# Norm factors by square root and reciprocal in place of logarithm and exponential, at the end and in the linear attention of a two-block model

## The reference, cut to what matters

```python
def rmsnorm(x, g):
    xf = x.astype(jnp.float32)
    y = xf * lax.rsqrt(jnp.mean(xf * xf, axis=-1, keepdims=True) + EPS)
    return (y * g.astype(jnp.float32)).astype(x.dtype)

# in bidirectional_gla, the linear attention (4 heads, 128 values each)
o = (fwd + bwd).astype(v.dtype).transpose(0, 2, 1, 3)
o = rmsnorm(o, norm_g) * jax.nn.silu(r.reshape(B, T, GLA_HEADS, GLA_DV))

# the end of second_block
h = h + sqrelu_mlp(h, ln_ff_g[l], w_ff1[l], w_ff2[l])
return rmsnorm(h, ln_final_g)
```

## Time and profile before

| | before |
|---|---|
| time, median of 3 runs | 2974.15 us (2974.0 to 2974.2) |
| profiled execution, its time | 2975.5 us |
| profiled execution, its span | 2973.7 us |
| mean granted TensorE clock | 0.99 of full speed |
| instructions | 42637 |

### The profile page before, as it was taken

One profiled execution on the slowest core, in us unless ns is written; L12 is line 12 of the kernel. 1 busy time (PEld: TensorE's weight loads), 2 busy tenths in 40 slices (PEclk: granted clock), 3 DMA queues, 4 the chain that ended last, 5 costly groups with the idle time before them and its releaser, 6 DMA issues.

```text
span 2973.7 us, 42637 instructions
## 1 busy us (share of the span) xinstructions
PE 2909.8 (98%) x16332; PEld 2413.5 (81%) x16332; DVE 1984.1 (67%) x3262; ACT 1441.8 (48%) x2411; POOL 467.7 (16%) x764
## 2 busy tenths in 40 slices
PE   9999999889999999999999999999999999999998
PEld 6888888778988887888878888777877788888887
DVE  6653246766775349999989852475654877778864
ACT  4552125887776126555444431375643544444432
POOL 0110004765554120000000010261012000000000
PEclk9999997999999999999999999999999999999999
DMA  4222231000000511333344332000101244464232
GB/s 150 73 84 71 85 114 43 2 1 2 2 2 7 207 43 64 114 114 114 114 160 157 116 111 92 28 2 36 43 30 72 104 165 168 157 241 156 99 114 71
DMA packets 85383, 262.14 MB, mean 88 GB/s; under 512 B 10448, under 2 KB 13648, under 8 KB 84800
## 3 DMA queue, kind: packets, MB, share of 16 engines
q1 hardware_dynamic: 74208, 219.29, 20.3%
q0 software_dynamic: 10976, 40.15, 3.8%
HBM read 187.58 MB, written 66.06 MB: 85 GB/s over the span
## 4 chain that ended last, share of the span: by engine, by line
PE 89%; DVE 4%; ACT 4%; issue 2%; POOL 0%; DMA 0%; SPq 0%; ACTq 0%; DVEq 0%; POOLq 0%
PE PS L256 33%; PE PS L3136 23%; PE PS L3158 12%; PE PS L919 3%; PE PS L933 3%; PE PS L905 2%; PE PS L904 2%; PE PS L280 1%; PE PS L1563 1%; PE PS L1598 1%; PE PS L1585 1%; ACT P_SHORT L1003 1%; PE PS L956 1%; PE PS L3187 1%; ACT PT L1013 1%
## 5 line engine op out<-in xcount | busy, mean ns | idle before, releaser
L223 ACT CAST WHI<-RAW 128x1024 fp32r<-128x1024 f32 x100 | 104.8, 1049 | 589.4 <-PE PS L256 569.6
L228 DVE TENSOR_TENSOR WLO<-RAW,WHI 128x1024 fp32r<-128x1024 f32 x102 | 125.5, 1231 | 361.4 <-ACT WHI L223 360.1
L256 PE MATMUL PS<-HLO,WHI 128*128 128x512 f32 x992 | 306.2, 390 | 0.0
L3136 PE MATMUL PS<-XSH_T,PWH 128*128 128x512 f32 x596 | 233.1, 391 | 5.4 <-DVE PWL L2396 2.4
L3136 PE MATMUL PS<-XSH_T,PWL 128*128 128x512 f32 x596 | 231.9, 389 | 0.0
L3136 PE MATMUL PS<-XSL_T,PWH 128*128 128x512 f32 x596 | 231.9, 389 | 0.0
L3158 PE MATMUL PS<-DXH,PWH 128*128 128x512 f32 x560 | 218.1, 389 | 1.4 <-DVE DXL L2620 1.3
L256 PEld LDWEIGHTS PS<-HLO,WHI 128*128 128x128 f32 x992 | 186.5, 188 | 39.2
L3158 PE MATMUL PS<-DXL,PWH 128*128 128x512 f32 x560 | 217.9, 389 | 0.0
L3158 PE MATMUL PS<-DXH,PWL 128*128 128x512 f32 x560 | 217.9, 389 | 0.0
L3136 PE MATMUL PS<-XSH_B,PWL 128*128 128x512 f32 x456 | 177.4, 389 | 0.0
(11 more groups left out here) (443 smaller groups left out, 7225.6 us busy)
## 6 DMA issues: line engine op xcount, KB each, us to landing
W<-in_w SPq DMA_DIRECT2D x57, 1024.0 KB, 6.4
RAW<-in_w SPq DMA_DIRECT2D x104, 512.0 KB, 3.3
hidden<-W SPq DMA_DIRECT2D x54, 512.0 KB, 2.8
DXR<-hidden_t SPq DMA_DIRECT2D x20, 1024.0 KB, 5.1
DXR<-hidden SPq DMA_DIRECT2D x15, 1024.0 KB, 5.1
hidden_t<-W SPq DMA_DIRECT2D x24, 512.0 KB, 3.3
hidden_t<-T SPq DMA_DIRECT2D x16, 512.0 KB, 3.1
PLAIN_RAW<-hidden SPq DMA_DIRECT2D x14, 512.0 KB, 4.2
```

Source lines behind the costliest of these rows:

```text
L223: nc.scalar.copy(WHI[:, slot, :], RAW[:, slot, :]).then_inc(w_hi, 1)
L228: nc.vector.tensor_tensor(WLO[:, slot, :], RAW[:, slot, :], WHI[:, slot, :].bitcast(F32), ALU.subtract).then_inc(w_lo, 1)
L256: last = nc.tensor.matmul(o[:, half], w[:, slot, cols], x(k)[:, half], start=(k == 0 and w is WHI and x is hi), stop=(done and k == kcs - ...
L3136: last = nc.tensor.matmul(c.banks[q % 2][b], wt[n % 4][:, cols], xt[x][:, k, :], start=(opens and k == 0 and xt is c.xsh and wt is c.pwh), ...
```

## The change

At both places Ln and Exp are replaced by one square root on ScalarE and a reciprocal on VectorE. In linear attention the reciprocal goes ahead of the norm's multiplication, in place, 128x8 elements, and a wait of VectorE for itself follows (`seq`). At the end it goes to the head of `dve_end_scale`, 128x512 or 128x256 elements. The other norms of the kernel keep Ln and Exp.

```diff
@@ act_gla
             act.wait_ge(gl_ms, h + 1)
-            nc.scalar.activation(ORS[:, h, :], OSUM[:, h, :], ACT.Ln, scale=1.0 / GLA_DV, bias=EPS_T[:, 0:1])\
+            nc.scalar.activation(ORS[:, h, :], OSUM[:, h, :], ACT.Sqrt, scale=1.0 / GLA_DV, bias=EPS_T[:, 0:1])\
                 .then_inc(gl_root, 1)
-            act.wait_ge(gl_root, 2 * h + 1)
-            nc.scalar.activation(ORS[:, h, :], ORS[:, h, :], ACT.Exp, scale=-0.5).then_inc(gl_root, 1)
@@ dve_gla_norm
-        dve.wait_ge(gl_root, 2 * h + 2)
+        dve.wait_ge(gl_root, h + 1)
+        seq(dve, nc.vector.reciprocal(ORS[:, h, :], ORS[:, h, :]))
@@ act_ff2_down
             act.wait_ge(mean_done, 4 + i + 1)
-            nc.scalar.activation(LN_B[:, a0:a1], SIDE[0][:, a0:a1], ACT.Ln, bias=EPS_T[:, 0:1]).then_inc(ln_done, 1)
-            act.wait_ge(ln_done, 4 + i + 1)
-            nc.scalar.activation(RSTD[4][:, a0:a1], LN_B[:, a0:a1], ACT.Exp, scale=-0.5).then_inc(rstd_done, 1)
+            nc.scalar.activation(LN_B[:, a0:a1], SIDE[0][:, a0:a1], ACT.Sqrt, bias=EPS_T[:, 0:1]).then_inc(ln_done, 1)
@@ dve_end_scale
         a0, a1 = END_COLS[i]
+        dve.wait_ge(ln_done, 4 + i + 1)
+        nc.vector.reciprocal(RSTD[4][:, a0:a1], LN_B[:, a0:a1]).then_inc(rstd_done, 1)
         dve.wait_ge(rstd_done, 4 + i + 1)
```

## The result

| | before | after |
|---|---|---|
| time, median of 18 runs each | 2975.26 us (2972.35 to 2978.66) | 2980.57 us (2979.0 to 2985.05) |
| ratio | | 1.0021, 95% interval 1.0015 to 1.0027 |
| profiled execution, its time and its span | 2975.5, 2973.7 us | 2982.74, 2981.0 us |
| instructions | 42637 | 42625 |

By the ratio the kernel is slower by 0.21%: 0.0021 x 2975.26 = 6.2 us, with an interval of 4.5 to 8.0 us. The two medians lie 5.3 us apart, a quotient of 1.0018 that is inside the same interval. The forecast was +6.2 us and 2980.4. That 2980.4 and 2980.57 lie so close is in part chance, since the kernel before ran at 2975.26 in these runs, not at 2974.15; the number to compare is the difference. That there is a loss is clear of the noise. The traces show where it comes from.

The account below looks back on a forecast made before the run. At the end VectorE was taken as a second path only 0.7 us shorter than the chain of waits. +6.28 there and -0.1 in linear attention gave +6.2, from 2974.15 to 2980.4 us, range 2979.0 to 2982.4.

Parts of the forecast that it names:

- VectorE as the second path: At the end, VectorE is a second path only 0.7 us shorter than the chain of waits.
- rival 5: Nothing at the end sits on VectorE: reciprocal (1.74) replaces load and Exp (1.75), no difference, 2974.1; chance 0.02.
- One sign: At the end, VectorE without idle time of over 0.1 us from 2957 on.
- The price of a reciprocal: On VectorE, 6.2 ns an element: 3.33 us for 128x512, 1.74 us for 128x256.
- R: Sum of the end's three reciprocals on VectorE: 6.81 us.
- Rivals 1 and 3: End reciprocals: the first, they stream, 2975.0, no difference, chance 0.07; the other, steep price, 8.71 us in sum, 2982.3, chance 0.07.
- The re-laid row of VectorE: At the end, VectorE's steps plus reciprocals put the first of the last eight scalings at 2973.62 against 2967.34: +6.28 us.
- The root of piece 2: At the end, ScalarE's last square root is ready by 2969.0, and VectorE asks for it at about 2971.8.
- The 2.1 us: At the end, time from the last mean's second square to the root's end, less the start of the load.
- SyncE's stores: Last eight stores go at SyncE's pace, 0.5 us each, before and after, so the stretch behind the first scaling stays as long.
- Linear attention: Reciprocal for load and Exp in each head: +0.2 in head 1, -0.3 in head 3, nothing in others; sum -0.1 us.
- rival 2: TensorE's clock at `within(3)` comes back to the upper level: +4.9, 2979.1, chance 0.09; converse, a second low stretch: 2981.6, 0.05.

Follow-up runs that it names:

- Experiment 5: Only the end changed to square root and reciprocal, with piece 0's reciprocal moved between piece 1's residual additions, where VectorE was idle; against experiment 1: ratio 1.0018.
- Experiments 3: Kernel before, with square root and reciprocal only in the last piece of the end (piece 2): ratio 0.9999.
- experiment 6: Kernel before, with one ScalarE instruction (Abs_reciprocal_sqrt) giving the factor at both places, no Exp and no reciprocal: ratio 1.0001.
- experiment 4: Kernel before, with reciprocals of 16 to 1024 elements and copies of 256 to 1024 added behind VectorE's last scaling: 2990.12 us.
- experiments 6 to 8: First experiment 6; then it with VectorE's scalings spread (ratio 0.9999); then that with ScalarE issuing every other store of the last piece (0.9992, 2972.92 us).
- experiment 2: Kernel after with the end put back to Ln and Exp, so only linear attention is changed: ratio 1.0001, 2976.02 us.
- experiment 1: Kernel after with linear attention put back to Ln and Exp, so only the end is changed: ratio 1.0021, 2981.96 us.

## Why the prediction was right, point by point

**VectorE as the second path** was right, and it carries everything. It had 0.7 us of room, it got 6.85 us of reciprocals, and the last scalings moved by 6.37. Experiment 5 shows it from the other side: where VectorE had idle time, a reciprocal of 3.35 us cost 0.6. Experiments 3 and 6 rule out the reading by the chain of waits alone (rival 5): a swap that is even on the chain lost 1.2 us, and a chain shorter by 1.7 us moved the last scalings by no more than VectorE's 0.58 and the end of the span by nothing. One sign was missed: VectorE was to have no idle time of over 0.1 us, and it waited 0.22 for a square.

**The price of a reciprocal** was taken as 6.2 ns an element from the medians at two and eight elements, 32 to 256 times narrower. The true line is 153 ns + 6.25 ns. Predicted R = 6.81, measured 3.35 + 1.75 + 1.75 = 6.85. Rivals 1 and 3 are out by experiment 4. The repeat count of 8 in the Trainium skill ("VectorE: DVE Perf Modes", section "First, the fixed hardware budget"), read as eight cycles an element, would be 8.3 ns, an estimate from that page; the 6.25 measured don't agree, and the measurement decides.

**The re-laid row of VectorE** gave +6.28 and was +6.37. Of the 0.09, 0.04 is the price and 0.06 the step from the residual of piece 2 to its addition (0.97 against 0.91, less rounding): the square came 0.45 behind the start of its residual as before, but the addition followed the square's end by 0.10 where 0.04 had been put. The root of piece 2 was expected 2.8 us ahead of VectorE and was 2.66 ahead. The 2.1 us that the prediction gives from the second square to the root's end are 1.78 by its own rows (2965.57 - 2963.79), and 2.41 were measured: TensorE had been idle for 4.24 us, its clock then fell (granted 0.67 from 2968 to 2970, against 1.00 from 2964 to 2966 before), and the last sum took it 1.65 us in place of 1.10. The slack hides all of this.

**SyncE's stores** were described as going at the same pace before and after, which missed that before they also had a backlog from piece 1. It is worth 0.15 us here, and it is why experiment 6 gained nothing at the end of the span.

**Linear attention** was right in size and in both its terms: +0.2 for head 1 (0.24 measured), -0.3 for head 3, -0.1 to -0.2 in all. VectorE's two waits for Exp, 1.89 us each in heads 2 and 3, were real, and all but 0.3 us of them lay beside products of TensorE.

**The clock** (rival 2) did not decide this comparison, since it fell at `within(3)` in both profiled executions: 3.28 us before and 3.60 after. But that it would be as before was luck, not insight. It fell in 1 of the 5 profiled executions with Ln and Exp in linear attention, in 1 of the 2 with square root and reciprocal there, and in all 3 with the single instruction of experiments 6 to 8. Ten executions are too few to say whether a change there makes the fall likelier, so this rival is not closed. Were the fall likelier by a half, that would be worth 0.6 to 0.8 us (half of the 1.3 to 1.6 that it cost in the traces, an estimate); experiment 2, whose interval is 5 us wide, can't tell.

The result on the scale of the runs is +6.2 us by the ratio and +5.3 by the medians, against +6.2 predicted. That the ratio agrees to the decimal is chance within its interval of 4.5 to 8.0, and the 0.72 that the prediction gave to a loss of over 0.2% is neither borne out nor refuted by it. The traces put the difference at 6.22 for the end less 0.1 to 0.2 for linear attention, with the clock's share open.

## What to carry to other kernels

The chain of waits names the path that ended last, not the one next to it. Before work is moved from one engine to another, lay out the receiving engine's timeline from the last point where it was idle, and count its idle time: in this kernel what it had less of than the moved work was lost, whatever the chain got back. A reciprocal on VectorE is fine on a statistic of eight elements (0.2 us) and expensive on a factor spread over a wide tile (3.35 us for 512 elements, five times a multiplication of the same shape), so keep it on the narrow side of a broadcast, or let one ScalarE instruction give the reciprocal root (how exact that one is was not measured here).

## What the runs showed that I had not expected

- TensorE's clock after the same 1.47 us of idleness ahead of `within(3)`: granted 0.50 (1.2 GHz) in 5 of 10 executions (16 matmuls in 3.28 to 3.63 us), the full 1.00 in the other five (2.02 us). The idle time ahead of `turn_back(1)` doesn't sort them either: 0.56 us in the kernel before, where the clock fell, and in experiment 1, where it didn't. What decides it stays open. With one kernel's trace such a stretch looks like a cost of the code. Two us in the kernel before, in which the clock comes back (a mean of 0.66; the earlier trace rows has the two us ahead), and two us in experiment 1, where that code is the same:

```profile
2240.00:2242.00 2.00, 2.00 (x28) 1.64 (x29) 1.70 (x2) 1.20 (x3) 0.00 (x0) 0.66 0.00 0
```

```profile
2238.00:2240.00 2.00, 1.63 (x14) 1.66 (x15) 1.35 (x2) 0.59 (x2) 0.00 (x0) 1.00 0.00 0
```

- The same kernel's runs scatter by 10 us (2969.7 to 2979.9 for the kernel before in experiments 5 to 8), while the end stretch, read from an anchor in the trace, repeats to 0.01 us: 20.28 and 20.29 in the two kernels with the changed end, 13.91 before and in experiment 2 (2967.07 - 2953.16). A change of 1 to 2 us can be judged in the trace and not in the runs.
- After a square root, squares and copies needed no new table: one load at each place for all roots. Between Ln and Exp a load of 1.283 us stood every time at the two places in the kernel before.
